# Second down projection with tokens stationary, weights moving, and a per-token norm

## The reference

```python
h = rms_norm(x, norm_ffn_pre[layer])
u = h @ w_up[layer]                               # 1024 -> 2 * 2816
u = causal_depthwise_conv(u, ffn_conv_w[layer], ffn_conv_b[layer])
u_gate, u_val = jnp.split(u, 2, axis=-1)
f = jax.nn.gelu(u_gate, approximate=True) * u_val
y = f @ w_down[layer]                             # 2816 -> 1024
x = x + rms_norm(y, norm_ffn_post[layer])         # y * rsqrt(mean(y*y) + eps) * gain
```

## Time and profile before

| | us |
|---|---|
| median of 3 runs (lowest, highest) | 1596.03 (1595.37, 1596.34) |
| the profiled execution's own time | 1595.91 |
| its span, first to last instruction | 1594.1 |
| TensorE matmuls busy in the span | 1569.2 |
| VectorE busy | 1108.0 |
| ScalarE busy | 563.5 |

### The profile page before, as it was taken

The page is one execution under the profiler, slowest core; times in us unless marked ns, Lnnn a source line. Parts: engine busy times, 40 slices in busy tenths (PEclk is TensorE's granted clock), DMA queues, the critical chain, the costliest instruction groups (busy, mean ns, idle before and its releaser), DMA issues.

```text
span 1594.1 us, 24870 instructions
## 1 busy us (share of the span) xinstructions
PE 1569.2 (98%) x9650; PEld 1422.7 (89%) x9650; DVE 1108.0 (70%) x1593; ACT 563.5 (35%) x808; POOL 42.1 (3%) x114
## 2 busy tenths in 40 slices
PE   7999999999999999999999999999999999999997
PEld 7999999999999988998888898878889888888887
DVE  5434566689888842288999998954657899898224
ACT  5123323442222222253233444477335422222221
POOL 4100000000000000000001011000000000000000
PEclk9999999999999999999999999999999999999999
DMA  5522322232322233232333232222231323323332
GB/s 192 139 89 93 92 67 93 67 104 83 92 92 92 92 106 99 86 113 93 94 105 87 80 99 86 81 81 79 93 96 64 119 93 96 101 92 95 109 110 83
DMA packets 45001, 152.46 MB, mean 96 GB/s; under 512 B 5947, under 2 KB 8023, under 8 KB 44928
## 3 DMA queue, kind: packets, MB, share of 16 engines
q1 hardware_dynamic: 42912, 147.26, 29.3%
q0 software_dynamic: 2016, 4.16, 1.2%
HBM read 149.25 MB, written 4.51 MB: 96 GB/s over the span
## 4 chain that ended last, share of the span: by engine, by line
PE 78%; DVE 17%; ACT 2%; issue 1%; DMA 1%; SPq 0%; DVEq 0%
PE ps L546 66%; PE ps L556 8%; DVE work L1742 6%; DVE wlo L1379 4%; PE ps L877 1%; DVE work L1505 1%; DVE work L1508 1%; ACT whi L982 1%; DVE tmp L1444 1%; DVE work L1540 1%; PE ps L928 1%; DMA raw<-w_dram 1%; DVE stage L1496 1%; DVE res L1457 1%; PE ps L828 1%
## 5 line engine op out<-in xcount | busy, mean ns | idle before, releaser
L546 PE MATMUL ps<-xh,whi 128*128 128x258 f32 (+2 forms) x1848 | 505.8, 325 | 10.3 <-DVE wlo L1379 8.4
L546 PE MATMUL ps<-xh,wlo 128*128 128x258 f32 (+2 forms) x1848 | 501.2, 323 | 0.0
L546 PE MATMUL ps<-xl,whi 128*128 128x258 f32 (+2 forms) x1848 | 500.5, 322 | 0.0
L1379 DVE TENSOR_TENSOR wlo<-raw,whi 128x1024 fp32r<-128x1024 f32 x272 | 331.6, 1219 | 152.2 <-ACT whi L982 151.7
L982 ACT ACTIVATE whi<-raw 128x1024 fp32r<-128x1024 f32 x272 | 287.1, 1057 | 406.3 <-DMA raw<-w_dram 384.3
L546 PEld LDWEIGHTS ps<-xh,whi 128*128 128x128 f32 x1848 | 310.1, 190 | 37.1 <-issue 11.5
L546 PEld LDWEIGHTS ps<-xh,wlo 128*128 128x128 f32 x1848 | 309.1, 189 | 26.9
L546 PEld LDWEIGHTS ps<-xl,whi 128*128 128x128 f32 x1848 | 310.0, 189 | 25.8 <-issue 0.2
L1742 DVE SCALAR_TENSOR_TENSOR work<-cin,vecs,work 128x512 f32<-128x512 f32 x240 | 180.2, 751 | 6.9
L546 PE MATMUL ps<-fh,wlo 128*128 128x512 f32 x264 | 102.7, 389 | 0.0
L546 PE MATMUL ps<-fl,whi 128*128 128x512 f32 x264 | 102.7, 389 | 0.0
(11 more groups left out here) (237 smaller groups left out, 2231.7 us busy)
## 6 DMA issues: line engine op xcount, KB each, us to landing
raw<-w_dram SPq DMA_DIRECT2D x272, 512.0 KB, 3.5
bias_copies_dram<-bias_rows_dram POOLq DMA_DIRECT2D x12, 192.0 KB, 3.9
res<-x_dram SPq DMA_DIRECT2D x8, 264.0 KB, 6.3
out_dram<-res SPq DMA_DIRECT2D x16, 128.0 KB, 1.9
dftp<-dftp_dram POOLq DMA_DIRECT2D x1, 550.7 KB, 4.4
bias<-bias_copies_dram POOLq DMA_DIRECT2D x4, 128.0 KB, 2.5
bias<-bias_copies_dram POOLq DMA_DIRECT2D x8, 64.0 KB, 2.8
vecs<-vec_dram SPq DMA_DIRECT2D x1, 364.0 KB, 8.0
```

Source lines behind the costliest of these rows:

```text
L546: last = pe.matmul(ps[:, bank, 0:b - a], w[:, slot, cols], xx[:, k, a:b], start=start and n == 0, stop=stop and n == 2)
L1379: dve.tensor_tensor(wlo[:, slot, :], raw[:, slot, :], whi[:, slot, :].bitcast(F32), ALU.subtract).then_inc(w_split, 1)
```

## The change

The second down projection is turned over. Its stationary operand is now a block of 128 inner channels x 128 tokens of `fh` or `fl`, and the weights move: 512 output channels per matmul. The output has tokens on the partitions. Four token blocks t and two channel halves h fill the eight PSUM banks, `ps[:, 2 * t + h]`. A piece of weights now is 128 inner channels x all 1024 outputs, and there are 22 pieces instead of 24 (270 in the stream instead of 272).

The order of the products (`down_by_tokens` of the tensor engine): pieces 0 and 1 for blocks 2 and 3, then for blocks 0 and 1; pieces 2 to 17 one after the other, each for all eight banks; then, bank by bank, the last four pieces 18 to 21 together (`TOGETHER = KFF - 4`), and a bank is done after each 12 matmuls.

The norm's sum over channels becomes a sum along the row: ACT squares a bank and accumulates (`accum_out`) in one pass; DVE adds the two halves, ACT takes the root, DVE the reciprocal, and one DVE pass per half multiplies by it (a number per partition) and adds the residual. DVE multiplies by the gain before, from `gain_rows`, a copy of the gain on all partitions that POOL loads in the second block. There is a store of 256 KB for each bank, eight in all.

Since the residual must have tokens on the partitions too, TensorE transposes `res` in the up stage: the loop of `tiles_after_norm` is cut at turns 5 and 8, and at each cut 16 transposes of 128 x 128 go into banks 4 to 7 (`turn_residual`); ACT copies them back into `res` (`keep_turned`). POOL's part in the last additions and `first_sums` and `last_sums` are gone.

```diff
+TURNED_AT = (5, 8)
+TOGETHER = KFF - 4
...
+            for n in range(CHUNKS // SLOTS_W * SLOTS_W, CHUNKS):
+                sp.wait_ge(w_used, n - SLOTS_W + 1)
+                sp.dma_start(raw[:, n % SLOTS_W, :], w_in[n]).then_inc(w_landed[n % SLOTS_W], 16)
+            for t in range(QB):
+                for h in range(2):
+                    sp.wait_ge(out_ready, 2 * t + h + 1)
+                    sp.dma_start(out[t, :, h * SEQ:(h + 1) * SEQ].rearrange("n (k c) -> n k c", k=KD // 2),
+                                 token_rows(t, h)).then_inc(stored, 16)
...
+            pool.wait_ge(operand_ready, READY["attn"])
+            pool.dma_start(gain_rows[:, :], bass.AP(gain_in.tensor, 0, [[0, P], [1, D]])).then_inc(rows_landed, 16)
...
+            def down_by_tokens():
+
+                def products(n, t, h):
+
+                    pe.wait_ge(w_split, C0["down2"] + n + 1)
+                    pe.wait_ge(operand_ready, READY["f2"] - KFF + n + 1)
+                    rows, cols = slice(t * P, (t + 1) * P), slice(h * SEQ, (h + 1) * SEQ)
+                    for m, (f, w) in enumerate(((fh, whi), (fl, whi), (fh, wlo))):
+                        last = pe.matmul(ps[:, 2 * t + h, :], f[:, n, rows], w[:, n % SLOTS_W, cols],
+                                         start=n == 0 and m == 0, stop=n == KFF - 1 and m == 2)
+                    return last
+
+                for pieces, blocks in (((0, 1), (2, 3)), ((0, 1), (0, 1))):
+                    for t in blocks:
+                        for n in pieces:
+                            for h in range(2):
+                                if t < 2 and n == 0:
+                                    pe.wait_ge(tile_read, T0["down2"] - 3 + 2 * t + h)
+                                last = products(n, t, h)
+                last.then_inc(w_used, 2)
+                for n in range(2, TOGETHER):
+                    for t in range(QB):
+                        for h in range(2):
+                            last = products(n, t, h)
+                    last.then_inc(w_used, 1)
+                for t in range(QB):
+                    for h in range(2):
+                        for n in range(TOGETHER, KFF):
+                            last = products(n, t, h)
+                        last.then_inc(block_done, 1)
+
+            def turn_residual(n):
+
+                if n:
+                    pe.wait_ge(turned_kept, 4 * n)
+                for t in range(2 * n, 2 * n + 2):
+                    for h in range(2):
+                        for c in range(KD // 2):
+                            last = pe.transpose(ps[:, 4 + 2 * (t % 2) + h, c * P:(c + 1) * P],
+                                                res[:, h * KD // 2 + c, N_META + t * P:N_META + (t + 1) * P],
+                                                ident[:, :])
+                        last.then_inc(turned, 1)
...
+                for t in range(QB):
+                    for h in range(2):
+                        act.wait_ge(block_done, 2 * t + h + 1)
+                        act.activation(squared[:, 2 * t + h, :], ps[:, 2 * t + h, :], ACT.Square,
+                                       accum_out=token_sums[:, t, h:h + 1]).then_inc(block_summed, 1)
+                    act.wait_ge(token_total_ready, t + 1)
+                    act.activation(token_root[:, t:t + 1], token_total[:, t:t + 1], ACT.Sqrt, bias=small[:, 2:3],
+                                   scale=1.0 / D).then_inc(token_root_ready, 1)
...
+                for t in range(QB):
+                    dve.wait_ge(block_summed, 2 * t + 1)
+                    gain(t, 0)
+                    dve.wait_ge(block_summed, 2 * t + 2)
+                    dve.tensor_tensor(token_total[:, t:t + 1], token_sums[:, t, 0:1], token_sums[:, t, 1:2], ALU.add) \
+                       .then_inc(token_total_ready, 1)
+                    gain(t, 1)
+                    dve.wait_ge(token_root_ready, t + 1)
+                    step(dve.reciprocal(token_inv[:, t:t + 1], token_root[:, t:t + 1]))
+                    after_step()
+                    for h in range(2):
+                        rows = token_rows(t, h)
+                        dve.scalar_tensor_tensor(
+                            out=rows, in0=gained[:, t % 2, h * SEQ:(h + 1) * SEQ].rearrange("p (k c) -> p k c", c=P),
+                            scalar=token_inv[:, t:t + 1], in1=rows, op0=ALU.mult, op1=ALU.add).then_inc(out_ready, 1)
```

More of the change, by code:

```diff
@@ L455, in _ @@
                       .then_inc(w_landed[s], 16)
[L456 to L466, removed]
+            for n in range(CHUNKS // SLOTS_W * SLOTS_W, CHUNKS):
[6 more added lines that the diff above has]
+                                 token_rows(t, h)).then_inc(stored, 16)
+            sp.wait_ge(stored, 32 * QB)
         @block.gpsimd
@@ new lines, in tiles_after_norm @@
+            def tiles_after_norm(phase, tiles, operand, spans, points=()):
+                rotate = 4
+                ends = (len(PAIRS_OF[phase]) // 4,) + points + (tiles // 4,)
+                for n, (first, end) in enumerate(zip(ends, ends[1:])):
+                    if n:
+                        turn_residual(n - 1)
+                    with pe.Fori(first, end) as it:
+                        for s in range(4):
+                            one_piece_tile(phase, it * 4 + s, s, s % rotate, it * 4 + (s - rotate + 1), operand, spans)
@@ L753, in sum_channels @@
                                          ones[:, 0:1], start=True, stop=True)
[L754 to L771, removed]
                 last.then_inc(sums_ready, 1)
@@ L794, in ffn @@
                 norm_tiles_by_halves(up, operand, halves_, READY[h_name] - 2 * KD, before, norm, row)
-                tiles_after_norm(up, 2 * KFF, operand, row)
-                down_tiles(dn, after, f_name)
+                tiles_after_norm(up, 2 * KFF, operand, row, TURNED_AT if up == "up2" else ())
+                if dn == "down1":
+                    down_tiles(dn, after, f_name)
+                else:
+                    down_by_tokens()
             all1 = [(0, L1 // 2), (L1 // 2, L1)]
@@ L1094, in staged, with keep_turned, down_by_tokens @@
                 act.activation(dst, src, func).then_inc(tile_read, 1)
+            def keep_turned(n):
+                for t in range(2 * n, 2 * n + 2):
+                    for h in range(2):
+                        act.wait_ge(turned, 2 * t + h + 1)
+                        act.activation(token_rows(t, h), ps[:, 4 + 2 * (t % 2) + h, :].rearrange("p (k c) -> p k c", c=P),
+                                       ACT.Copy).then_inc(turned_kept, 1)
+            def down_by_tokens():
+                for n in range(3, KFF):
+                    w_to_hi("down2", 0, n)
+                for t in range(QB):
[6 more added lines that the diff above has]
+                                   scale=1.0 / D).then_inc(token_root_ready, 1)
             def ffn(up, dn):
@@ L1112, in ffn @@
                     up_body(it)
-                with act.Fori(unrolled, KFF // 2) as it:
-                    up_body(it)
+                ends = (unrolled,) + (TURNED_AT if up == "up2" else ()) + (KFF // 2,)
+                for n, (first, end) in enumerate(zip(ends, ends[1:])):
+                    if n:
+                        keep_turned(n - 1)
+                    with act.Fori(first, end) as it:
+                        up_body(it)
                 act.preload_act_table(ACT.Sqrt)
+                if dn == "down2":
+                    down_by_tokens()
+                    return
                 act.wait_ge(tile_read, T0[dn])
-                post = "post1f" if dn == "down1" else "post2f"
-                gain = "g_ffn_post" if dn == "down1" else "norm_ffn_post_2"
+                post = "post1f"
+                gain = "g_ffn_post"
                 for m in range(6):
@@ L1136, in second_down_half @@
                 piece_used(dn, (20, 23)[i])
[L1137 to L1138 removed]
+                half_tile("post1f", 6 + i, 1, (3, 7)[i], down, "g_ffn_post")
             def out_tile(phase, post, n, mix, gain):
@@ L1345, in _ @@
             ffn("up2", "down2")
[L1346 to L1351, removed]
         @block.vector
@@ L1935, in _ @@
             inverse_of_res("up2", "pre2f", SEQ)
[L1936 to L1952, removed]
+            ffn("up2", "down2", 0, "ffn_conv_w_2", "ffn_conv_b_2", None, "f2")
 def _weight_tiles(w, first=0, count=None):
@@ L2054 @@
             for name, v in arrays.items()]
-    out = nc.dram_tensor("out_dram", (P, KD, SEQ), mybir.dt.float32, kind="ExternalOutput").ap()
+    out = nc.dram_tensor("out_dram", (QB, P, D), mybir.dt.float32, kind="ExternalOutput").ap()
     two_block_kernel(nc, *args, out)
     r = _run(nc, [arrays], core_ids=[0])
-    got = r.results[0]["out_dram"]
-    return np.ascontiguousarray(got.transpose(2, 1, 0)).reshape(1, SEQ, D)
+    return np.ascontiguousarray(r.results[0]["out_dram"]).reshape(1, SEQ, D)
```

63 lines of the change are left out of this document (38 added, 25 removed).

## The result

The changed kernel takes 1597.98 us (median of 22 executions), the kernel before 1595.33 (22 executions beside them). The ratio is 1.0016, with a 95% interval of 1.001 to 1.0022: 2.65 us more. The interval lies above 1, but the difference is smaller than the 0.2% (3.2 us) from which this measurement tells a change from none. The forecast was 1597.2. One execution of the changed kernel took 6013 us and is left out of the ratio.

The account below looks back on a forecast made before the run. TensorE, busy 98% of the span, was taken as the bound. Terms -2.6 + 4.1 + 3.4 - 4.0 = +0.9, plus 0.2 for wait ends, on the median 1596.03 gave 1597.1, rounded up to 1597.2 us; range 1594.0 to 1600.4.

Parts of the forecast that it names:

- Part 1: Second down stage: 528 matmuls of 512 columns take 119.9 us instead of 122.47, a gain of 2.6 us.
- Part 2: End of the down stage: TensorE stands 4.1 us for piece 21, whose slot is freed late by piece 17.
- Part 3: Up stage: 32 added transposes on TensorE, overlapping and covered by nothing, cost 3.4 us.
- the rival with the full duration: Up stage: transposes do not overlap and cost 8.8 us instead of 3.4, giving 1602.5 us; chance 0.06.
- Part 4: After the last matmul: norm, addition and store take 6.0 us instead of 9.96, a gain of 4.0 us.
- The clock holds: Down stage: TensorE waits about 4 us for piece 21 without its clock falling; chance 0.48, no cost added.
- the rival in which it falls: Behind the wait for piece 21: matmuls run at half rate, at most 3.0 us lost, 1600.1 us; chance 0.30.

Follow-up runs that it names:

- e1: The changed kernel with only the last three pieces (19 to 21) taken together bank by bank instead of four; 1592.35 us, ratio 0.998 to the kernel before.
- e3: The changed kernel without the 32 transposes and ACT's copies back, the loop still cut; 1594.54 us, ratio 0.9995 to the kernel before.
- e2: The changed kernel with only the last two pieces taken together bank by bank instead of four; 1592.37 us, ratio 0.9981 to the kernel before.
- e7: The changed kernel with TensorE repeating piece 20's products, 18 matmuls, during the wait for piece 21; 1596.53 us, ratio 1.001 to the kernel before.
- e4: The changed kernel with each block taking pieces 18 to 20 for both banks before piece 21; 1594.13 us, ratio 0.9997 to the kernel before.
- e6: On top of e1, DVE's last addition and its store cut into two halves; 1592.43 us, ratio 0.9983 to the kernel before.

## Why the prediction was right, and the step that failed

**Part 1, the matmuls, -2.6: right.** Without the wait (e1) the stage takes 119.84, forecast 119.9, so 2.63 less than before. The activation as stationary operand costs nothing that shows: 528 matmuls at 0.2267 and the end of the last are 119.86.

**Part 2, the wait, +4.1: right.** The trace has 3.94 of idle time; from the start of the last matmul before it to the first behind it are 4.33, 4.10 more than usual. The chain shows the links that were added up: load 3.56, ACT 1.07, DVE 1.24, and from the end of the slot's last matmul (1562.97) to the first matmul behind the wait (1568.94) 5.97, where the forecast had 5.98. e1 shows that the missing lead of a slot is the cause: with one piece less at the end the wait is gone.

**Part 3, the transposes, +3.4: right,** 3.4 by e3's median, 3.57 by its trace; the cuts of the loop, for which the upper bound allowed 1 us each, cost nothing. Their starts are close and their durations overlap, so the rival with the full duration falls. ACT's copies are hidden.

**Part 4, the tail, -4.0: right,** 5.92 against 6.0 forecast. Its terms were off in opposite ways: DVE's path from the square to the last addition is shorter than forecast (3.0 behind the product instead of 3.4), the landing 0.1 longer, and the rest 0.5 instead of 0.3. The block's 3.3 us of DVE, which had to fit under the matmuls of the next block, are 2.79; at 5.44 of matmuls per block that did not matter, and at the 2.72 of e2 it decided that the tail grew by only 0.2.

**"The clock holds": wrong.** This is the step that failed: the forecast had 0.48 for a wait with the clock up, and 0.30 for the rival in which it falls. It fell, and the sum had nothing for it. For its price the rival had 3.0 at most and a third of that as the milder case; the runs say 1.45 (e7 against the changed kernel, by medians) to 1.8 (the trace). I had set the one pause of 1.6 us that left the rate as it was the earlier trace rows against the half rate at the start of the span and the clock of 0.50 at its end; the two pauses of 4 us (here and in e3) brought the half clock, as the rival said. The rule of the Trainium skill that the prediction set beside this rival ("TensorE: Matmul & The Clock Gate", "Why this matters for your kernels") is what happened here: the granted clock was 0.51 from 1 us behind a gap of 3.94.

The four terms as measured in the traces give -2.63 + 4.10 + 3.57 - 4.04 = +1.00, against +0.9 forecast. The clock adds 1.76 (the rest of 125.70 - 119.84), the stretch ahead of the sixteenth tile -0.38, which together is the 2.4 between the two spans. The -0.38 is scatter: in e1 and e2, whose instructions are the same up to there, that stretch ends at 1303.92 and 1302.53.

That the time itself came within 0.8 of the forecast is in part luck. The change was forecast at +1.2 and measured at +2.65, short by about what the clock cost. But the forecast was set on the median of three executions of the kernel before, 1596.03, and the 22 that stand beside the result have 1595.33; this 0.7 covered half of the miss.

## What to carry to other kernels

Work that is put together at the end of a stage needs its operands together too: count, for the last pieces, how many matmuls lie between the release of a slot and the first use of what is loaded into it; here one piece less at the end (three instead of four) turns 1.0016 into 0.998. A pause of TensorE costs its length and, where it brings the half clock, the slow matmuls behind it, here 1.45 to 1.8 us behind a pause of 3.9; the one profiled execution of e4 shows a pause of 1.8 us that escaped this, and whether such a pause always does stays open. A tail that is hidden under the matmuls of the next block stays hidden only while these last longer than the block's own chain, so measure that chain as the distance of its repeats and not as the sum of its durations.

## What the runs showed of the hardware

- Transposes of 128 x 128 in float32, 272 ns each, start about 0.11 us apart when 16 stand in a row (1.91 from first start to last end); two groups cost 3.4 us by e3's median and 3.57 by its trace.
- A store of 128 KB in pieces of 512 bytes did not land sooner than one of 256 KB: 2.4 against 2.3 (e6). The store before the change, 128 KB in its own layout, took 1.9.
- Behind the pause the clock did not fall at once: in the changed kernel the first starts behind it were still 0.23 to 0.37 apart, and the half rate lasted from about 1570.0 to 1573.4.
